# Weight buffers with a pitch of 544 bytes per chunk and a skew of 64 bytes per ring slot, in a kernel that streams split float32 weights through TensorE

## What is computed

```python
def trunk(x, ...):
    mix, cb, rs = mixer(rmsnorm(x, norm_mix_g), ...)   # x @ w_in (2048 x 7168), short convolution
    x = x + mix                                        # and retention by heads, then @ w_out
    x = x + peer(rmsnorm(x, norm_ffn_g), w_q, sub_keys, u_tab, v_tab)
    return rmsnorm(x, norm_final_g), ...

def peer(h, ...):                                      # 16,384 experts of one neuron each
    q  = h @ w_q                                       # 8 heads, two halves of 128
    sc = q . sub_keys                                  # 128 keys for each half
    # the best 16 of each half, the best 16 of their 256 sums: index and softmax gate
    act = gelu(h . u_tab[idx]);  w = gate * act
    return sum(w * v_tab[idx])
```

## Time and profile before

| | before |
|---|---|
| time, median of 3 runs | 2123.25 us (2122.4 to 2123.27) |
| span in the profiled execution | 2120.7 us |
| TensorE busy | 2099.2 us, 99% |
| VectorE busy | 1441.5 us, 68% |
| ScalarE busy | 963.0 us, 45% |
| DMA, mean rate over the span | 197 GB/s |

### The profile page before, as it was taken

The page is one execution under the profiler, slowest core; times in us unless marked ns, Lnnn a source line. Parts: engine busy times, 40 slices in busy tenths (PEclk is TensorE's granted clock), DMA queues, the critical chain, the costliest instruction groups (busy, mean ns, idle before and its releaser), DMA issues.

```text
span 2120.7 us, 46483 instructions
## 1 busy us (share of the span) xinstructions
PE 2099.2 (99%) x18585; PEld 2087.6 (98%) x18585; DVE 1441.5 (68%) x2700; ACT 963.0 (45%) x1343; POOL 68.4 (3%) x94
## 2 busy tenths in 40 slices
PE   8999999999999999999999999999999999999997
PEld 8999999999999999999999999999999999999997
DVE  8888876568888677755656656565645556666665
ACT  6666533444534344443434344443434344444444
POOL 1111000000000000000000000000000000000000
PEclk9999999999999999999999999999999999999999
DMA  8666555654455556675556565565656566656653
GB/s 296 222 217 216 189 180 182 199 176 152 159 188 179 179 189 213 207 245 184 195 198 212 187 213 196 195 204 194 212 188 205 174 216 203 215 202 201 205 180 123
DMA packets 115175, 418.39 MB, mean 197 GB/s; under 512 B 13600, under 2 KB 14112, under 8 KB 114752
## 3 DMA queue, kind: packets, MB, share of 16 engines
q1 hardware_dynamic: 100800, 365.29, 52.2%
q0 software_dynamic: 9888, 34.47, 5.0%
q10 hardware_dynamic: 4320, 16.22, 2.0%
HBM read 391.55 MB, written 24.29 MB: 196 GB/s over the span
## 4 chain that ended last, share of the span: by engine, by line
PE 98%; DVE 1%; ACT 0%; DMA 0%; issue 0%; DVEq 0%; SPq 0%; ACTq 0%
PE bank L929 32%; PE bank L930 31%; PE bank L931 31%; PE bank L1102 2%; PE bank L1057 1%; DVE wlo L1181 0%; PE bank L1002 0%; DMA acc<-xT 0%; DVE acc L1871 0%; PE bank L1013 0%; PE bank L1009 0%; PE bank L977 0%; PE bank L987 0%; PE bank L961 0%; DVE outer L1273 0%
## 5 line engine op out<-in xcount | busy, mean ns | idle before, releaser
L1181 DVE TENSOR_TENSOR wlo<-raw,whi 128x1024 fp32r<-128x1024 f32 x688 | 830.5, 1223 | 500.4 <-ACT whi L634 496.5
L634 ACT CAST whi<-raw 128x1024 fp32r<-128x1024 f32 x688 | 710.2, 1048 | 630.8 <-PE bank L931 624.7
L929 PE MATMUL bank<-xhi,whi 128*128 128x264 f32 x3200 | 911.5, 285 | 0.0
L930 PE MATMUL bank<-xlo,whi 128*128 128x264 f32 x3200 | 906.7, 283 | 0.0
L931 PE MATMUL bank<-xhi,wlo 128*128 128x264 f32 x3200 | 906.5, 283 | 0.0
L930 PEld LDWEIGHTS bank<-xlo,whi 128*128 128x128 f32 x3200 | 603.1, 188 | 0.0
L929 PEld LDWEIGHTS bank<-xhi,whi 128*128 128x128 f32 x3200 | 602.6, 188 | 0.2 <-issue 0.2
L931 PEld LDWEIGHTS bank<-xhi,wlo 128*128 128x128 f32 x3200 | 600.1, 188 | 0.0
L929 PE MATMUL bank<-xghi,whi 128*128 128x264 f32 x1152 | 333.5, 289 | 9.5 <-DVE wlo L1181 9.5
L929 PE MATMUL bank<-wexp_hi,whi 128*128 128x264 f32 x1152 | 328.0, 285 | 0.0
L930 PE MATMUL bank<-xglo,whi 128*128 128x264 f32 x1152 | 327.4, 284 | 0.0
(11 more groups left out here) (216 smaller groups left out, 1125.0 us busy)
## 6 DMA issues: line engine op xcount, KB each, us to landing
raw<-halves SPq DMA_DIRECT2D x688, 512.0 KB, 3.4
hid<-gates ACTq DMA_DIRECT2D x30, 528.0 KB, 4.9
gates<-stage POOLq DMA_DIRECT2D x17, 768.0 KB, 7.1
s_old<-ret_state POOLq DMA_DIRECT2D x8, 512.0 KB, 7.4
vs_all<-values POOLq DMA_DIRECT2D x8, 512.0 KB, 5.6
ret_sample<-s_new POOLq DMA_DIRECT2D x8, 512.0 KB, 4.2
gates<-route_mem POOLq DMA_DIRECT2D x5, 768.0 KB, 7.4
acc<-xT SPq DMA_DIRECT2D x4, 528.0 KB, 6.3
```

The lines of the kernel that those rows point to most:

```text
L634: nc.scalar.copy(whi[:, s], raw[:, s]).then_inc(hi_done, 1)
L929: nc.tensor.matmul(out, whi[:, s, c], mh[c], start=start and c == 0, stop=False)
L930: nc.tensor.matmul(out, whi[:, s, c], ml[c], start=False, stop=False)
L1181: v.tensor_tensor(wlo[:, s], raw[:, s], whi[:, s].bitcast(F32), ALU.subtract).then_inc(lo_done, 1)
```

## The change

`whi` and `wlo` get a chunk pitch of 136 floats (544 bytes; `P + T % P` = 128 + 8) and 16 floats (64 bytes) more for each ring slot, so a slot takes 8 x 544 + 64 = 4,416 bytes. The views that all engines use keep their shape, 128 x 4 x 8 x 128. `raw` stays as it is. Each of the two buffers grows from 16,384 to 17,664 bytes on a partition, so all that is declared behind `whi` moves up, `wlo` by 1,280 bytes and the rest by 2,560. To make room, `onehot1` becomes a view of `pair`, and `route_mem` is declared with 8,320 floats in place of 8,448. No instruction is added, removed or moved on any engine; the operands of `hi_half`, `lo_half` and the first compare of a batch have another layout.

```diff
 RING = 4
 BANKS = 4
+
+PITCH = P + T % P
+SKEW = 16
...
 ROUTE = ((LEAD + 1) * GROUP - ROUTE_AT) * T
+LISTS = 8320
...
         raw = sb("raw", [P, RING, HALF, P])
-        whi = sb("whi", [P, RING, HALF, P], F32R)
-        wlo = sb("wlo", [P, RING, HALF, P], F32R)
+        def staggered(name):
+            flat = sb(name, [P, RING, HALF * PITCH + SKEW], F32R)
+            return flat[:, :, 0:HALF * PITCH].rearrange("p r (c m) -> p r c m", c=HALF)[:, :, :, 0:P]
+
+        whi, wlo = staggered("whi"), staggered("wlo")
...
-        route_mem = sb("route_mem", [P, ROUTE], F32, scope)
+        route_mem = sb("route_mem", [P, LISTS], F32, scope)
...
-        onehot1 = sb("onehot1", [P, GB, SPAN], BF16)
+        onehot1 = pair[:].rearrange("p a t -> p (a t)").bitcast(BF16)[:, 0:GB * SPAN].rearrange("p (t k) -> p t k", t=GB)
...
-                ch.did(equal(onehot1[:], iota16[:, half * SPAN:(half + 1) * SPAN], i1T, SPAN))
+                ch.did(equal(onehot1, iota16[:, half * SPAN:(half + 1) * SPAN], i1T, SPAN))
...
-                                           onehot1[:].rearrange("p t (a d) -> p t a d", d=2),
+                                           onehot1.rearrange("p t (a d) -> p t a d", d=2),
```

More of the change, by code:

```diff
@@ L317, in carve @@
                 at[0] += n
-                assert at[0] <= ROUTE
+                assert at[0] <= region.shape[-1]
                 names = " ".join("abcd"[:len(shape)])
```

## The result

The changed kernel takes 2125.53 us (median of 20 runs, 2124.72 to 2126.57) against 2122.8 of before (20 runs beside it): ratio 1.0014, interval 1.0007 to 1.002. It became 2.7 us slower, where 7.8 us were forecast to be won.

The account below looks back on a forecast made before the run. The prediction took the step between matmuls on a full TensorE (120.9 ns) as the bound. The fixed distance was to win 7.8 us and all else about nothing, so 2123.25 became 2115.5 us, range 2100 to 2131.

Parts of the forecast that it names:

- What bounds the kernel: Whole run: TensorE busy throughout, no waits to remove; 16,512 matmuls at 120.9 ns make 1,996 of 2,120.7 us.
- The pattern follows the distance of two streams: Split-weight matmuls: step varies with moving address minus weights address, modulo 256; mean steps ran from 116.6 to 128.4 ns.
- places: Matmul operands: moving address minus weights address, modulo 256 bytes, divided by 32, giving 0 to 7.
- The value taken for a fixed place: All 16,512 matmuls: 120.4 ns each, 7.8 us won; from below 26 us won, from above 43 us lost.
- the slide: Old layout: moving operand shifts 32 bytes per chunk against the weights; pass 0 follows it, averaging 121.6 ns against 120.6.
- Its own sign of being wrong: Third matmul of each chunk's three passes: a cost above 122 ns would show the prediction wrong.
- The rival "averages": Matmul steps: each address distance costs what the old kernel's table says; 1.7 us won, 2121.5 us; chance 0.19.
- C: Experiments' theory on matmul steps, not in the prediction: each fixed distance runs in a repeating cycle with its own mean.
- Bad places held fast: Slots 0 and 1 outside the x family: 123.5 and 122.5 ns, 7.3 us lost, 2130.5 us; chance 0.20.
- No effect: Matmul steps: ports independent, pattern from the moving address alone; time stays 2123 us; chance 0.12.
- Strided writes: ScalarE and VectorE writes of split weights in 512-byte pieces: covered by TensorE, nothing taken, 0.1 us on first two halves.
- The weights' start: Weight loads at odd multiples of 32 bytes: 1.4 ns each on 8,256 matmuls, 11.5 us lost, 2135 us; chance 0.08.

## Why the prediction was wrong

**What bounds the kernel** held: TensorE full, no waits, clock unchanged, and the step between matmuls the only thing that changed.

**The pattern follows the distance of two streams** held, and is now shown by the run with the weights 32 bytes on. Before, it was argued from two families alone. The rule of the Trainium skill ("TensorE: Matmul & The Clock Gate", step-by-step section) that loading the next weights takes nothing from the running matmul does not agree with these runs: with only the weights' addresses different, 16,512 matmuls take 1978, 2027 and 2050 us (places 2, 5 and 4). The rule of the Trainium skill ("SBUF — State Buffer", on who interferes with whom) that TensorE waits for no other engine agrees with the rows: the steps shown above repeat with a spread of 0.5 ns or less over 36 halves, beside the writes of ScalarE, VectorE and the DMA.

**The value taken for a fixed place** is the step that failed, and with it the whole 7.8 us. The prediction took 120.4 ns, the mean of pass 1, for every place, because "neither operand's place has changed" there: it put what pass 0 costs above that down to the slide, and let all three passes come down to it once the slide is gone. Without the slide pass 1 stayed low (120.2 ns), but pass 0 still averages 121.5 (121.6 before) and pass 2 went up from 120.7 to 121.6. Two streams that keep their distance do settle, but not at a common value: the cycles depend on the distance. The means are 119.8 ns at place 2, 120.6 at 3, 121 at 6, 120.4 to 121.5 at 7, 121.4 at 0, 122 at 1, 122.7 at 5, and 120.3 or 124.7 at 4. The skew then spreads the matmuls over all eight places, four for each family, and gives back their average, 121.09. The prediction had named an average, but as the rival with half the chance. Its bounds, 119.3 and 123.5, were nearly right; the dearer cycle of place 4 lies above the upper one. Its own sign of being wrong, pass 2 above 122, did not come (121.6 over all, 119.2 to 122.8 by slot and family). The 834 matmuls in a late window did not come either: there were 828 and 831.

**The rival "averages"** (T) was right on the outcome of no gain (-1.7 us against +3.2 measured) and on the signs of the families, but sized them by the table of before: it gave -8.1 and +6.4 us, measured were -2.2 and +5.4. All at place 2 tells it apart from C best: T had a loss there, 18 us were won. A table taken with the slide in it does not hold without the slide.

**"Bad places held fast"** was right for one of its two places: places 7 and 5 were to take 123.5 and 122.5 ns. Place 5 did (123.0 and 123.2); place 7 did not (120.8 and 120.4), and place 1, not named, lost as well (122.0).

**"No effect"** came nearer in time (2123) than the forecast, but not by its reason: the pattern is not that of the moving address alone.

**Strided writes, `onehot1`, `route_mem`** at nothing held: 1223 and 1047 ns unchanged, and the run with the old pitch gives the time of before.

**The weights' start**, the rival at 2135, is refuted by the shift of 32 bytes.

What stays open: why the distance modulo 256 bytes counts at all was not measured, nor what decides which of the two cycles of place 4 an interruption leaves behind. Places 1, 3 and 6 were seen only by slots, never with all matmuls there.

## What to carry to other kernels

When TensorE is full and its clock is steady, look at the starts of its matmuls: a step that repeats with the chunk's number and hardly spreads points to an address effect, and shifting one buffer by 32 bytes shows at no cost whether distance or address makes it. Removing the variation is not the same as removing the cost: fix the distance, measure every value of it, and give all operands the best one. Look at single stretches as well as at means, because a mean can hide two cycles. A skew that spreads them over all values buys the average. Here the pitch with no skew and all operands at place 2 won 18 us, 0.85%, where pitch and skew lost 2.7.

## What the runs showed of the hardware that was not expected

- The distance between the moving operand and the weights, modulo 256 bytes, changes the step of a 128 x 128 by 264 fp32r matmul: 119.8 ns in the mean with all matmuls at place 2, 122.7 at place 5 and 124.1 at place 4, or 1978, 2027 and 2050 us over 16,512 matmuls.
- At a fixed distance the steps don't become equal. They run in cycles of one to four chunks. In the changed kernel the mean steps by slot, chunk and pass run from 116 to 127 ns.
- The same addresses can hold two cycles: with all matmuls at place 4 most halves run at 124.7 ns and 54 in a row at 120.3, and a cycle changes only after other work on TensorE (or the start of the run).
- Writes of 512-byte pieces at a pitch of 544 bytes cost ScalarE and VectorE nothing that shows: 1047 and 1223 ns for 1,024 elements, as before.
